# A decoder block with expert retrieval: 64 of 256 tokens leave the dense expert products and take their chosen rows by indirect DMA

## What is computed

```
q = (h @ w_q).reshape(T, PEER_HEADS, PEER_KEY_DIM)
s1 = einsum('thd,kd->thk', qb[..., :half], k1)       # 128 scores each
s2 = einsum('thd,kd->thk', qb[..., half:], k2)
v1, i1 = top_k(s1, 16);  v2, i2 = top_k(s2, 16)
top, pos = top_k(v1[..., :, None] + v2[..., None, :], 16)
idx = take_along_axis(i1 * 128 + i2, pos)            # the chosen experts
g = softmax(top)
u = u_tab[idx];  vv = v_tab[idx]
act = gelu(einsum('thkd,td->thk', u, hb)) * g
ff = einsum('thk,thkd->td', act, vv)
x = x + gt_f * rms_norm(ff, g_post_ffn)
```

## Time and profile before

| | |
|---|---|
| median of 3 runs | 2123.53 us |
| the profiled execution's own time | 2123.66 us |
| its span, first to last instruction | 2121.9 us |
| PE busy, DVE busy, ACT busy | 96%, 65%, 39% of the span |
| granted PE clock, mean | 0.991 |
| moved by DMA | 492.06 MB, 232 GB/s over the span |

### The profile page before, as it was taken

How to read it: one execution, slowest core, us unless ns; L and a number is a source line. 1 busy time by engine, 2 the same in 40 slices (tenths; PEclk the granted TensorE clock), 3 DMA queues, 4 the chain that set the end, 5 groups by cost and what they waited for, 6 DMA issues and landing times.

```text
span 2121.9 us, 34149 instructions
## 1 busy us (share of the span) xinstructions
PE 2047.3 (96%) x12430; PEld 1801.5 (85%) x12430; DVE 1378.9 (65%) x2378; ACT 836.3 (39%) x1085; POOL 7.1 (0%) x17
## 2 busy tenths in 40 slices
PE   4999999979999999999999999989999999999997
PEld 4888885439999999998999999978888888888886
DVE  4668897666777777775666666645555555555555
ACT  3011223015444444444555555544444444444444
POOL 0000000000000000000000000000000000000000
PEclk9999999999999999999999999999999999999999
DMA  8996565987866666664555555556666666666665
GB/s 353 421 421 260 221 234 218 399 354 267 328 203 200 208 200 205 207 202 160 171 179 178 178 178 178 179 208 211 216 216 212 221 208 219 215 208 221 213 219 188
DMA packets 117197, 492.06 MB, mean 232 GB/s; under 512 B 13681, under 2 KB 14225, under 8 KB 96657
## 3 DMA queue, kind: packets, MB, share of 16 engines
q1 hardware_dynamic: 105984, 468.76, 62.9%
q10 hardware_dynamic: 11090, 22.49, 2.8%
q0 software_dynamic: 64, 0.02, 0.0%
HBM read 470.24 MB, written 20.98 MB: 232 GB/s over the span
## 4 chain that ended last, share of the span: by engine, by line
PE 90%; DMA 5%; DVE 3%; ACT 1%; issue 1%; ACTq 0%; DVEq 0%; SPq 0%
PE ps L843 35%; PE ps L1152 33%; PE ps L881 5%; PE ps L865 4%; PE ps L1043 4%; PE ps L1113 3%; PE ps L892 3%; DMA early<-in_w_front 3%; PE ps L992 2%; DVE early L1195 1%; DMA early<-in_w_ada 1%; DMA gsub<-in_g_subln 1%; DMA raw<-in_peer_wq 0%; PE ps L1034 0%; PE ps L971 0%
## 5 line engine op out<-in xcount | busy, mean ns | idle before, releaser
L324 DVE TENSOR_TENSOR w_lo<-raw,w_hi 128x1024 fp32r<-128x1024 f32 x544 | 666.4, 1225 | 578.3 <-ACT w_hi L628 577.3
L628 ACT ACTIVATE w_hi<-raw 128x1024 fp32r<-128x1024 f32 x544 | 576.8, 1060 | 944.7 <-PE ps L843 431.7
L843 PE MATMUL ps<-a_hi,w_hi 128*128 128x256 f32 x2048 | 591.8, 289 | 7.4 <-DVE w_lo L324 5.7
L843 PE MATMUL ps<-a_lo,w_hi 128*128 128x256 f32 x2048 | 580.4, 283 | 0.0
L843 PE MATMUL ps<-a_hi,w_lo 128*128 128x256 f32 x2048 | 580.4, 283 | 0.0
L843 PEld LDWEIGHTS ps<-a_hi,w_hi 128*128 128x128 f32 x2048 | 393.7, 192 | 9.3 <-DVE w_lo L324 6.1
L843 PEld LDWEIGHTS ps<-a_lo,w_hi 128*128 128x128 f32 x2048 | 394.1, 192 | 0.2 <-issue 0.2
L843 PEld LDWEIGHTS ps<-a_hi,w_lo 128*128 128x128 f32 x2048 | 393.5, 192 | 0.0
L1152 PE MATMUL ps<-w_lo,a_hi 128*128 128x512 f32 x1024 | 319.2, 393 | 6.1 <-issue 6.0
L1152 PE MATMUL ps<-w_hi,a_lo 128*128 128x512 f32 x1024 | 317.4, 391 | 0.0
L1152 PE MATMUL ps<-w_hi,a_hi 128*128 128x512 f32 x1024 | 317.2, 391 | 0.0
(11 more groups left out here) (203 smaller groups left out, 1768.7 us busy)
## 6 DMA issues: line engine op xcount, KB each, us to landing
raw<-in_peer_u SPq DMA_DIRECT2D x256, 512.0 KB, 3.7
raw<-in_peer_v SPq DMA_DIRECT2D x256, 512.0 KB, 3.5
early<-in_w_ada SPq DMA_DIRECT2D x60, 1024.0 KB, 10.7
early<-in_w_front SPq DMA_DIRECT2D x42, 1024.0 KB, 9.5
raw<-in_w_ada SPq DMA_DIRECT2D x20, 1024.0 KB, 9.9
raw<-in_peer_wq SPq DMA_DIRECT2D x32, 512.0 KB, 6.8
big<-in_w_gate_f SPq DMA_DIRECT2D x16, 1024.0 KB, 5.4
gel_saved<-stage ACTq DMA_DIRECT2D x64, 256.0 KB, 3.9
```

The costliest lines, as they stand in the source:

```text
L324: engine.tensor_tensor(w_lo[:, s % 2, part], ring[j % ph.ring][:, part], w_hi[:, s % 2, part].bitcast(F32), ALU.subtract)\
L628: act.activation(w_hi[:, s % 2, :], ring[j % ph.ring], ACT.Copy).then_inc(hi_ready, 1)
L843: done = pe.matmul(ps[:, b % 2, 0:T], w[:, half, k * P:(k + 1) * P], a[:, kc, :], start=kc == 0 and m == 0, stop=kc == KC - 1 and m == 2)
```

## The change

The last 64 tokens (TS) no longer take part in UP, ROUTE and DOWN, which keep the first 192 (TD). For the 64, the 128 chosen rows of each are spread over the 128 partitions, 64 rows in each (partition p holds half of the experts of token p mod 64). POOL fetches them by indirect DMA, 128 rows of 8 KB at a time: 64 gathers from a second, plain copy of the u table (`u_rows`), then 64 from the v table. DVE takes the dot product of each gathered u row with the token (`dot`) beside ROUTE's units, nine in a round, and adds each gathered v row times its weight into `acc` (`add_row`) beside DOWN's units, four in a round. The u rows have three buffers, the v rows four.

PH_UP's 8 rounds are now 4 of PH_UP and 4 of PH_MID; the search for the second token tile, which holds the 64, comes first, so that their indices are there after PH_UP. The masks of ROUTE are made for four tokens at once, both one-hot matrices by one DVE operation of 128x1024, and ACT scales one of the two by the softmax weight. DOWN is turned round: the v table is stationary, 128 columns at a time, and the 192 tokens move, so a unit has 24 matmuls with 192 columns. The result is then transposed in PSUM, and transposed back to tokens at the end, by PE (`turn_out`), where the two halves of `acc` are added with a product by `pair`. The multiplications for the gate row (`gate_row_out`) move from ROUTE's start to UP.

```diff
+TD = 192
+TS = T - TD
+SLICES = P // TS
-PH_UP = Phase(PH_WQ, EXPERT_BLOCKS // 16, "w" * 16)
-PH_ROUTE = Phase(PH_UP, EXPERT_BLOCKS // 16, "w" * 16)
+PH_UP = Phase(PH_WQ, EXPERT_BLOCKS // 32, "w" * 16)
+PH_MID = Phase(PH_UP, EXPERT_BLOCKS // 32, "w" * 16)
+PH_ROUTE = Phase(PH_MID, EXPERT_BLOCKS // 16, "w" * 16)
+USE, MASK, PUT = (1, 4, 6, 9, 12, 14), (0, 3, 6, 8, 11, 14), (3, 6, 8, 11, 14, 15)
+DOTS_AT = (1, 2, 4, 5, 7, 9, 10, 12, 13)
+SUMS_AT = (3, 6, 11, 14)
...
+            def gather(n, table, where, done):
+                gp.indirect_dma_start(where, None, table, bass.IndirectOffsetOnAxis(ap=row_ix[:, n:n + 1], axis=0))\
+                    .then_inc(done, 16)
+            gp.wait_ge(gate_f_saved, 16)
+            gp.wait_ge(row_ix_in, 32)
+            for n in range(ROWS):
+                if n >= 3:
+                    gp.wait_ge(row_used, n - 2)
+                gather(n, u_rows, got[n % 3], row_in[n % 3])
+            v_rows = peer_v.rearrange("b p d -> (b p) d")
+            for n in range(ROWS):
+                if n < 3:
+                    gp.wait_ge(row_used, ROWS - (ROWS - 1 - n) % 3)
+                elif n == 3:
+                    gp.wait_ge(split_used, PH_DOWN.s)
+                else:
+                    gp.wait_ge(v_row_used, n - 3)
+                gather(n, v_rows, got[n % 4], v_row_in[n % 4])
...
+            def scale_masks(g, i):
+                act.wait_ge(oh_masked, at(i, 6, g + 1))
+                for t in range(4):
+                    token = bass.ds(at(i, 24, 4 * g + t), 1)
+                    done = act.activation(masks[:, 1, t, :], masks[:, 1, t, :], ACT.Copy, scale=sel_T[:, 2, token])
+                done.then_inc(oh_ready, 1)
...
-                            done = pe.matmul(ps[:, b % 2, 0:T], w[:, half, k * P:(k + 1) * P], a[:, kc, :],
+                            done = pe.matmul(ps[:, b % 2, 0:TD], w[:, half, k * P:(k + 1) * P], a[:, kc, 0:TD],
...
-                    for tt in range(2):
-                        toks = slice(tt * P, (tt + 1) * P)
-                        for m, (a, w) in enumerate(((a_hi, w_lo), (a_hi, w_hi), (a_lo, w_hi))):
-                            for n in range(2):
-                                done = pe.matmul(ps[:, 4 * tt + 2 * (j % 2) + n, :], a[:, blk, toks],
-                                                 w[:, j % 2, n * 512:(n + 1) * 512],
-                                                 start=i is None and blk == 0 and m == 0, stop=False,
-                                                 skip_group_check=True)
+                    for n in range(UCH):
+                        c = (j % 2) * UCH + n
+                        for m, (w, a) in enumerate(((w_hi, a_hi), (w_hi, a_lo), (w_lo, a_hi))):
+                            done = pe.matmul(ps[:, c // 2, (c % 2) * TD:(c % 2 + 1) * TD], w[:, j % 2, n * P:(n + 1) * P],
+                                             a[:, blk, 0:TD], start=i is None and blk == 0 and c % 2 == 0 and m == 0,
+                                             stop=False, skip_group_check=True)
...
+            def turn_out(tt, g):
+                pe.wait_ge(f_put_act, max(g, 2 * tt + g // 2) + 1)
+                pe.wait_ge(f_put_dve, max(g, 2 * tt + g // 2) + 1)
+                if tt:
+                    pe.wait_ge(v_row_used, ROWS)
+                    pe.wait_ge(pair_made, 2)
+                    pe.matmul(ps[:, 4 + g, :], pair[:, :], acc[:, g * 512:(g + 1) * 512], start=True, stop=False,
+                              skip_group_check=True)
+                for n in range(4):
+                    cols = slice(n * P, (n + 1) * P)
+                    if tt:
+                        done = pe.matmul(ps[0:TD - P, 4 + g, cols], fT[:, 4 * g + n, P:TD], ident[:, :], start=False,
+                                         stop=n == 3, skip_group_check=True)
+                    else:
+                        done = pe.transpose(ps[:, g, cols], fT[:, 4 * g + n, 0:P], ident[:, :])
+                done.then_inc(f_turned, 1)
...
+            def make_masks(g, i):
+                if i is not None or g:
+                    dve.wait_ge(oh_used, at(i, 6, g))
+                dve.tensor_tensor(masks, iota[:, None, None, :].to_broadcast([P, 2, 4, P]),
+                                  sel_T[:, 0:2, bass.ds(at(i, 24, 4 * g), 4)].unsqueeze(3).to_broadcast([P, 2, 4, P]),
+                                  ALU.is_equal).then_inc(oh_masked, 1)
+            def dot(buf, arrived, out):
+                dve.wait_ge(row_in[buf], arrived)
+                dve.tensor_tensor_reduce(got[buf], got[buf], h_tok, 1.0, 0.0, ALU.mult, ALU.add, out)\
+                    .then_inc(row_used, 1)
...
             with dve.Fori(1, PH_ROUTE.n) as i:
                 for j in range(PH_ROUTE.per):
-                    one_hots(j, i)
+                    if j in MASK:
+                        make_masks(MASK.index(j), i)
                     lo(PH_ROUTE, j, i)
+                    if j in DOTS_AT:
+                        n = DOTS_AT.index(j)
+                        dot((n + 1) % 3, at(i, 48, 16 * ((n - 8) // 3 + 1)), dots_now[:, n:n + 1])
...
+            def add_row(n, i):
+                dve.wait_ge(v_row_in[n], at(i, 16, 16))
+                if i is None and n == 0:
+                    dve.tensor_scalar(acc, got[n], row_act[:, 0:1], None, ALU.mult).then_inc(v_row_used, 1)
+                else:
+                    dve.wait_ge(v_row_used, at(i, 4, n))
+                    dve.scalar_tensor_tensor(acc, got[n], row_act[:, bass.ds(at(i, 4, n), 1)], acc, ALU.mult, ALU.add)\
+                        .then_inc(v_row_used, 1)
```

More of the change, by code:

```diff
@@ L221, in build_block @@
         gate_f = early[:, 2048:4096]
+        got = [region(24576 + n * D, D) for n in range(3)] + [early[:, 6144:8192]]
         ones = sb("ones", [P, P])
@@ L770, in _ @@
[L770 to L776, removed]
+                if j == 6:
+                    for n in range(2):
+                        act.activation(h_twice[:, :, n * TS:(n + 1) * TS], h_full[:, :, TD:T], ACT.Copy)\
+                            .then_inc(twice_made, 1)
@@ new lines, in _ @@
+            for j in range(PH_MID.per):
+                up_unit(PH_MID, j, None)
+                if j == 2:
+                    act.wait_ge(expert_made, 1)
+                    for n in range(SLICES):
+                        act.dma_start(row_ix[n * TS:(n + 1) * TS, :],
+                                      expert_u[P - TS:P, n * ROWS:(n + 1) * ROWS]).then_inc(row_ix_in, 16)
+            with act.Fori(1, PH_MID.n) as i:
+                for j in range(PH_MID.per):
+                    up_unit(PH_MID, j, i)
@@ L803, in _ @@
             save_pair(EXPERT_BLOCKS - 1, None, 1)
+            act.wait_ge(dots_put, PH_ROUTE.n)
+            act.activation(dots[:, :], dots[:, :], ACT.Gelu).then_inc(row_gelu, 1)
             act.wait_ge(split_used, PH_DOWN.s)
@@ L1086, in _, with ahead_up @@
                         expert_scores(k)
+            def ahead_up(u, i):
+                if u == 6:
+                    pe.wait_ge(sc_copied, 8)
+                    pe.wait_ge(ada_used, 2 * KC)
+                    for g in range(4):
+                        done = pe.matmul(ps[:, 4 + g, :], ones[:, :], acc_last[:, g * 512:(g + 1) * 512], start=True,
+                                         stop=True)
+                    done.then_inc(gate_f_sum, 1)
+                if u == 12:
+                    pe.wait_ge(twice_made, 2)
+                    for g in range(4):
+                        pe.wait_ge(gate_f_made, g + 1)
+                        for kc in range(4):
+                            done = pe.transpose(ps[:, 4 + g, kc * P:(kc + 1) * P], h_twice[:, 4 * g + kc, :], ident[:, :])
+                        done.then_inc(h_turned, 1)
             for n in range(PH_UP.s_per // 2):
-                product(PH_UP, n, None)
+                product(PH_UP, n, None, ahead=ahead_up)
                 if n == 0:
@@ L1161, in _ @@
                 down(i)
+            def turn_out(tt, g):
[14 more added lines that the diff above has]
+                done.then_inc(f_turned, 1)
+            for half in range(2):
+                for tt in range(2):
+                    for g in range(2):
+                        turn_out(tt, 2 * half + g)
         @block.vector
@@ new lines, in all_experts @@
+            def all_experts(ph, row0):
+                base = count[0]
+                for q in range(2):
+                    experts(ph, q, None, base, row0)
+                with dve.Fori(1, ph.n) as i:
+                    for q in range(2):
+                        experts(ph, q, i, base, row0)
+                count[0] = base + 2 * ph.n * CHAIN_STEPS
+                dve.wait_ge(vec, count[0])
+            all_experts(PH_UP, 0)
+            link(dve.scalar_tensor_tensor(expert_f, idx1[:, 0:PEER_HEADS, :], float(KEYS), idx2[:, 0:PEER_HEADS, :],
+                                          ALU.mult, ALU.add))
```

247 lines of the change are left out of this document (150 added, 97 removed).

## The result

The changed kernel takes 2190.94 us (median of 4 runs, 2185.54 to 2194.0) against 2123.48: the ratio is 1.0315 (95% interval 1.0293 to 1.0336), slower by some 67 us. The forecast was 2180, range 2080 to 2245.

The account below looks back on a forecast made before the run. PE was taken to bound the expert stages, with ACT and DVE one step behind; UP -24, ROUTE +16, DOWN +54 and the tail +7 make +53 on 2123.66 us, so 2177, said as 2180, range 2080 to 2245.

Parts of the forecast that it names:

- case A: The forecast itself, chance 0.45: the weight load floors a 192-column matmul at 111.6 ns; 2177 us in all.
- UP: Term for eight rounds of UP and MID: the shorter unit takes 3.0 us off each round, -24 us.
- ROUTE: Term for eight rounds: DVE becomes the bound at 53.7 us, late loads add 1.3, 55.0 a round, +16 us.
- the end: Tail term: PE transposes and sums the output after the last product, so the last gating ends later, +7 us.
- DOWN: Term for sixteen rounds: four row sums on DVE stop PE, 47.4 us a round against 43.95, +54 us.
- B: Rival on the matmul's price, chance 0.25: 192 columns cost what 256 do, 120.0 ns; 2232 us in all.
- C: Rival, chance 0.15: columns set the matmul's price, 93.3 ns; the loop and DVE keep most of the gain; 2087 us.
- E: Rival, chance 0.04: a narrow matmul falls back to full precision's price, 325 ns; about 4,700 us in all.
- The window formula: DVE work w behind a subtraction stops PE (unit P) w + 3.69 - 2P; DOWN's row sums 0.66 or 1.58 us.
- the 85% that I had named as a sign: Sign for ROUTE in the profile after: DVE busy above 85%, with idle PE released by DVE.
- Rival D: Chance 0.08: gathers don't overlap, 7.8 us each one after another, a ROUTE round of 70 us; 2297 us in all.
- the sign of 10 us for each: Sign in the profile after: POOL's gathers land within 10 us.

Follow-up runs that it names:

- e1: The changed kernel with UP's matmuls cut to 128 moving columns and DOWN's to 160: 2956.7 us, one run.
- e7: The kernel before with UP and ROUTE products over 192 of the 256 tokens and nothing else: 2080.11 us, ratio 0.9795.
- e2: The changed kernel with each row sum in DOWN over 64 of its 2048 columns, gathers kept: 2119.9 us, ratio 0.9986.
- e5: The changed kernel, complete, with each DOWN row sum in two halves behind different units, none beside make_group or low_group: 2119.4 us, ratio 0.9984.
- e4: The changed kernel with an 8 KB plain transfer in place of each u-row gather, dot products kept whole: 2186.96 us, ratio 1.031.
- e8: The kernel before with DOWN turned round and all 256 tokens moving, 24 matmuls a unit instead of 12: 2161.03 us, ratio 1.0184.
- e6: e5 with ROUTE's dot products in halves too, eighteen in a round, complete computation: 2084.38 us, ratio 0.982.
- e9: The changed kernel with only DOWN's matmuls narrowed, UP left at 192, in two runs at 160 and 176 columns: 2742.86 and 2740.21 us, one run each.

## Why the prediction was right

The forecast's mechanism, case A, is what the runs show, and the sum came out 14 to 17 us low (2177 against 2190.94, or +53 against +70.3 of span). By stages the misses are larger: UP came out 17 us above its term and ROUTE 6 below, the end and DOWN 2 each above, and 2 us stand before UP, where the sum has nothing. That UP and ROUTE missed in opposite ways is luck.

*The matmul's price.* 111.6 ns was taken, 111.5 measured, and it is a floor: e1 has the same spacing at 128 columns. The reason given for it, two cycles of the load path for each weight column, stays a reading that no run tests: nothing here has a matmul without its load. Nor is 107 ns a floor of every load: in the kernel before, the first two loads of some transposes (L941, 128 x 128) start 60 ns apart. B (120 ns), C (93 ns) and E (full precision) are out by the spacing alone, and e7 shows it without the rest of the change.

*The window formula.* The stops of 0.66 and 1.58 us a row sum summed to 4.5 a round: a round measured 47.38 against 47.4, and the two sorts of stop 0.7 and 1.6 us, twice each. e2 and e5 each take the 70 us away, one by less work and one by smaller pieces elsewhere, with the gathers there in both, so DVE's pieces are the cause and the gathers' bytes are not. How much of it is size and how much is place is known from the formula alone, which the two sorts of stop bear out.

*ROUTE.* The round of 55.0 us came out at 55.02, but the reason was half wrong, and that it fits so closely is luck. I had 53.7 from DVE and added 1.3 for loads that land late. e4 took the gathers' DMA away and the round stayed: all of 55.0 is DVE and its order. From the subtraction of unit 1 (1073.33) to that of unit 14 (1119.17) I had 41.7 us of DVE's work and two waits for ACT of 1.5; it took 45.8, with four waits of 1.3, one in the unit behind each mask, where ACT also has the mask to scale. The first of them:

```profile
1083.65 1.23 DVE L354 TENSOR_TENSOR w_lo<-raw,w_hi 128x1024 fp32r<-128x1024 f32 x1 [1.27 <-ACT w_hi L678]
```

DVE's share was 83% and not above the 85% that I had named as a sign. The stage's total was +9.9, not +16: the sum counted eight rounds of dots where there are seven (7 x 2.02 = 14.1), and the gate row's products, 3.44 us, went to UP. The last 0.8 us was not taken apart.

*UP, the step that was mis-sized.* -24 was foreseen, -6.7 measured, 17 us less. The rounds gave what they should within a bit: 46.1 - 43.69 is 2.4 a round, 19 in all, where 3.0 was taken, since full DVE windows cost more than 0.1 us each; that is 5 us of the 17. The rest is what the sum had at zero. The gate row's 3.46 us of products (611.07) and its DVE work moved here, where PE stood from 619.87 to 627.12, while at ROUTE's start PE still waits, because ACT now waits there for `row_gate` to land (965.37) before it goes on. And the first three gathers made PE wait for a weight load, which by the comparison with e4 cost 5.7 us, of the piece of 11.32 us at 792.08. I had looked at the gathers' bytes in ROUTE only, and at whether the gathers are late, not at what three of them at once do to the weights behind them.

*The end.* +9.4 against +7: PE turns and sums from 2170.28 to 2180.3, 10.0 us where 9.7 were counted. But the sum let the last gating end with PE, and it ends at 2181.83, because DVE waits for ACT's squares in between, which end themselves at 2182.19:

```profile
2181.14 0.69 DVE L1788 TENSOR_TENSOR big<-ps,early 128x512 f32<-128x512 f32 x1 [1.38 <-ACT big L910]
```

*Rival D* (gathers that don't overlap) is out: nine land in a round of 55 us at a median of 9.2 us each (the row below, of 1066 to 1121), so they do overlap, and e4 shows them to cost nothing in ROUTE. A single one is slower than either of the prediction's two figures, 4.4 and 7.8 us, and over the whole run it takes 5.5 to 13.7 us, so the sign of 10 us for each held for the median only.

```profile
big<-in_u_rows,row_ix POOLq DMA_INDIRECT x9, 9.2
```

C's second half, that the loop and DVE would have kept most of a cheaper matmul, was not tried, since no width gave one.

What the change could have brought is in e7 and e8: 42 us from the narrower products of UP and ROUTE, and a DOWN that with its turn gives 17 at best (16 x (43.95 - 42.9)). DVE's large pieces then took 70 in DOWN and some 35 in ROUTE. The change had a gain in it, and e6 gets it with the same work cut smaller.

## What to carry to other kernels

Before narrowing a matmul, find the width below which its spacing no longer falls: here 192 columns cost 111.5 ns and 128 cost the same, and a loop turned to narrow operands pays for having twice as many matmuls. Look at the granted clock of the narrow version too. On an engine that feeds the bound one in a fixed rhythm, it is the longest piece between two deliveries that counts, not its load: compare each piece with the time from one delivery to the next less the delivery's own, and cut what does not fit, or move it, which was worth 107 us here with none of the work left out. A new transfer is to be weighed at its first burst and against the loads queued behind it, not only by its bytes per round; and the length of a DMA piece in the chain is not what it costs (11.32 us there, 5.7 in time).

## What the hardware showed that I had not expected

In the runs with narrower matmuls the granted clock did not hold. At 192 columns it fell at stops too (0.57 in the row below, after PE stood for 2.07 us), but rose again while the same matmuls went on, in UP and after DOWN's pause. At 176 and at 160 it stayed at 0.50 for all of DOWN, with a spacing of 213 ns instead of 111.5, and at 128 it fell from 1.00 to 0.50 at a stop in the middle of UP and did not rise again in that stage. The changed kernel and e9 with 176 columns are 550 us apart by 16 columns; the narrow runs were taken once each, but all three show it.

```profile
805.00:810.00 5.00, 4.21 (x20) 4.21 (x20) 4.02 (x18) 1.06 (x1) 0.00 (x0) 0.57 0.81 269
```

PE counts as 100% busy in the windows at 0.50 (and before the fall as 99%), so its busy share does not tell; the clock's column does. Why the clock was granted in the one and not in the others was not settled. The matmul's own duration fell only from 283 to 276 ns from 256 to 192 columns, though a quarter of its columns went, and at 128 it is still 0.27 to 0.28 us.
